# A gather for four heads of 32 tokens, folded by TensorE into 32 output partitions

## The chip, the cores and the metric

One Trainium2 chip, one of its cores, one launch of one program. The time is the device time of that core in microseconds (us). The engines are PE (TensorE, with its weight loads shown apart as PEld), DVE (VectorE), ACT (ScalarE), POOL (GpSimd, which here issues the gathers) and SP (SyncE, which here streams weights and stores results). All of them share 16 DMA engines.

## The reference, cut to what matters

Two transformer blocks run on 512 tokens of width 1024, in float32. The change lies in the end of the second block, a layer of single-neuron experts:

```python
def peer(h, w_query, sub_keys, u_tab, v_tab):        # h [512, 1024], tables [16384, 1024]
    q = (xb @ w_query).reshape(TOKEN_BLOCK, P_HEADS, 2, P_HALF)     # 8 heads, 2 halves of 128
    s = einsum('thpk,hpnk->thpn', q, sub_keys)                      # 128 keys for each half
    sv, si = lax.top_k(s, 16)
    cand = sv[:, :, 0, :, None] + sv[:, :, 1, None, :]              # 16 x 16 candidates
    fv, fpos = lax.top_k(cand, 16)                                  # 16 experts for each token and head
    g = softmax(fv)
    act = gelu(einsum('td,thkd->thk', xb, u_tab[eidx]))             # one dot product for each pick
    return einsum('thk,thkd->td', g * act, v_tab[eidx])             # weighted sum of 128 rows for each token
```

Each of the 512 tokens takes 8 heads x 16 picks = 128 experts, and each pick reads one row of `u_tab` and one of `v_tab` (8 KB together, since the two tables lie side by side). That is 65,536 rows or 537 MB, fetched by 512 gathers of 128 rows.

## The kernel before

The first block runs over all 512 tokens. The second block runs in two halves of 256 tokens, a = 0 and a = 1, and each half goes through the same stages: norm (n1), projections (in2a, in2b), two kinds of attention (mls, dif), output projection (out2), norm (n2), query projection with key scores (pq), and parking of x in DRAM.

The picks of half a can only begin when its key scores exist, at the end of its pq stage. So the 256 gathers of the first half are worked off during the stages of the second half. `picks(a, stage, j)` says how many picks each engine is to have passed before step j of a stage; `PER_US` sets the pace, and `LAST_PICK` = 212 is where the count stops. After the last stage the remaining 300 picks run alone. Every engine executes its program in order, so that a pick's instructions stand between fixed instructions of the stages.

One gather (a "pick", n = 0 to 511) works like this before the change. The 128 tokens of one tile (t = n // 128) sit in the 128 partitions, and pick n brings for each token the row of one head and rank:

- POOL issues the indirect DMA into a row buffer (line 1740). There are 4 buffers for the first 16 picks, 6 up to pick 271, then 8. It waits until the previous user of the buffer is done.
- DVE forms the dot products of 1024 columns with the token's activations (`dot`, line 1559).
- ACT applies Gelu (line 1246) and multiplies by the gate (line 1247).
- The value rows are added with that weight. Even picks (and the first 16) are added by DVE (`value`, line 1573, into `acc`). Odd picks go to PE (line 1053), which needs the weight on a diagonal: ACT makes a 128x128 diagonal (line 1253), and PE multiplies it with the rows in two matmuls of 512 columns, accumulating in PSUM banks 6 and 7. DVE follows its dot products by 1, 2 or 3 picks (`lag_of`); in the stages PE follows by 3 (`BEHIND_PE`).
- After each tile DVE adds both sums, the gate of the block and x, normalizes and lets SP store (`last`, lines 1581 to 1596).

The scores come from PE at line 1162, one head at a time as soon as its two query columns exist. The choice of experts is DVE's: `pick_keys` (lines 1506 to 1518), `pick_pairs` (1523 to 1528), `pick_experts` (1534 to 1544), `pick_gates` (1550, 1551). In half a, `pick_keys` for 14 of the 16 pairs of tile and head stands behind the first 14 picks, one each.

Every fp32 matmul of the program shows in the trace as two MATMUL and two LDWEIGHTS records.

Of the kernel before, what the change touches and what calls it, by code (L numbers as in the profile page):

```python
# [31 lines left out]
P = 128  # L32
# [19 lines left out]
NDIAG = 3  # L52
# [12 lines left out]
def lag_of(n):  # L65
    return 1 if n < NARROW else 2 if n < WIDE else 3


def on_pe(n):
    return n >= NARROW and n % 2 == 1  # L70


TURN, PE_BEFORE, DVE_BEFORE = [0] * NPICK, [0] * (NPICK + 1), [0] * (NPICK + 1)
EXP_AT, ROOT_AT, FETCH_AT, LAST_AT = 9, 14, 1, (3, 6, 8, 10, 16)
PREVIOUS, _seen = [None] * NPICK, {}
for _n in range(NPICK):
# [4 lines left out]
    PE_BEFORE[_n + 1] = PE_BEFORE[_n] + on_pe(_n)  # L81
    DVE_BEFORE[_n + 1] = DVE_BEFORE[_n] + (not on_pe(_n))

STAGES2 = [("n1", 1, 10.0), ("in2a", 17, 3.6), ("mls", 18, 2.5), ("in2b", 12, 3.6), ("dif", 26, 2.2), ("out2", 8, 3.6),
           ("n2", 1, 14.0), ("pq", 20, 3.6), ("park", 1, 4.0)]
# [54 lines left out]
CONSTS = [("ident", 128), ("mask", 512), ("rope", 512), ("sel", 512), ("iota", 16)]  # L140
# [14 lines left out]
def build(nc, ap, out):  # L155
    with ExitStack() as ctx:
        park_x = nc.dram_tensor("park_x", (T, P, D), F32, kind="Internal").ap()
        park_kv = nc.dram_tensor("park_kv", (P, 8 * HALF), F32, kind="Internal").ap()
# [8 lines left out]
        ARENA = 50000  # L167
        whole = sb("whole", [P, ARENA])
        ring = [whole[:, i * BLK:(i + 1) * BLK] for i in range(2)]
        xT = whole[:, 2 * BLK:3 * BLK].rearrange("p (k n) -> p k n", k=KD)  # L170
# [79 lines left out]
        wexp = place(58, 2, NSLOT)  # L250
# [3 lines left out]
        diag = place(62.5, NDIAG, P)  # L254
# [8 lines left out]
        h2tok = place(118, 2, D)  # L263
        acc = place(126, 2, D)
# [87 lines left out]

        def block_arrived(pe, n):
# [7 lines left out]
        def norm_act(act, name, src, n, dst=None, shift=None, ready=None):  # L361

            (b, k), (square, root, _) = NORM0[name], norm_tiles(name)
            for c in range(n):
# [4 lines left out]
                act.activation(square[:, c % 2, :], src(c), ACT.Square).then_inc(nrm_sq, 1)  # L369
# [27 lines left out]
        def norm_dve(dve, own, name, src, n, dst, gain):  # L397
# [7 lines left out]
            for c in range(n):  # L405
                dve.scalar_tensor_tensor(out=dst(c), in0=src(c), scalar=gain(c), in1=root,
# [484 lines left out]
        x_pe, x_parked, x_loaded = sem("x_for_parking"), sem("x_parked"), [sem("x_loaded0"), sem("x_loaded1")]  # L891
# [6 lines left out]
        v_dve, v_pe = sem("values_added_dve"), sem("values_added_pe")  # L898
# [31 lines left out]
        def _(sp):  # L930
# [12 lines left out]
            for t in range(T):  # L943
                sp.wait_ge(fin_ok, t + 1)
                sp.dma_start(out[t * P:(t + 1) * P, :], acc[:, t % 2, :]).then_inc(stored, 16)
# [4 lines left out]
        def _(pe):  # L950
# [91 lines left out]
            def value(n):  # L1042
                if not on_pe(n):
                    return
# [814 lines left out]
```

## Time and profile before

| | |
|---|---|
| median of 3 runs | 3017.92 us (3017.64 to 3023.72) |
| the profiled execution | 3018.04 us, its span 3015.9 us |
| PE busy | 2308.3 us (77%) |
| DVE busy | 1719.9 us (57%) |
| ACT busy | 895.3 us (30%) |
| POOL busy | 655.0 us (22%) |
| gathers and the modulation weights, queue q0 | 587.24 MB, 48.8% of the DMA engines' span |

The page's slices show three regions. Up to about 1400 us the first block and the first half of the second keep PE at 9 tenths while DMA is mostly idle. From about 1450 us all engines share the work and DMA stands at 7 to 9 tenths. In the last quarter PE falls to 5 and 6, DVE stands at 8 and DMA at 9 tenths. DMA's busy share counts the mean of 16 engines; PE's clock is the granted share of full speed. "x" in a row is the number of instructions, and what stands in brackets or behind a bar is the idle time of the engine before them with whoever ended it.

### The profile page before, as it was taken

Reading aid. Unit: us, or ns where it says so; the run is one execution under the profiler, and the core shown is the slowest. Engines: PE = TensorE matmul, PEld = TensorE weight load, DVE = VectorE, ACT = ScalarE, POOL = GpSimd, SP = SyncE. Lnnn points to the kernel's source line nnn. Section 1 sums busy time; section 2 is a strip of 40 time slices with the busy share of each in tenths; the row PEclk is TensorE's granted clock in tenths of the full one; section 3 lists DMA queues with packets and bytes.
Section 4 is the critical chain, followed back from the end, with each engine's and each line's share of the span. In section 5 each row is a group of like instructions: output and inputs, shape, how many; then the busy total and the mean of one; then the engine's idle time right before and its main releaser. Section 6 shows DMA issues by size and latency. Waiting matters only on the chain. (4 is left out here: it accounts for less than half of the span.)

```text
span 3015.9 us, 21942 instructions
## 1 busy us (share of the span) xinstructions
PE 2308.3 (77%) x6878; PEld 1251.0 (41%) x6878; DVE 1719.9 (57%) x3546; ACT 895.3 (30%) x2307; POOL 655.0 (22%) x540
## 2 busy tenths in 40 slices
PE   4999999999999999888475787777754356555555
PEld 2475654644444448667343453445411111111111
DVE  5422226312114314224886867778767888898887
ACT  1012322301000002222256528533322233333332
POOL 0000000000000000000132333333343255545553
PEclk8989989999999998979687797889866677767786
DMA  8520002012117522225598897799998699999998
GB/s 347 205 84 28 29 28 84 29 61 78 70 69 284 189 84 84 94 88 195 196 358 332 325 409 304 311 361 367 379 377 322 237 422 420 413 407 420 411 420 335
DMA packets 93376, 728.23 MB, mean 241 GB/s; under 512 B 10320, under 2 KB 10832, under 8 KB 13264
## 3 DMA queue, kind: packets, MB, share of 16 engines
q0 software_dynamic: 77184, 587.24, 48.8%
q1 hardware_dynamic: 12960, 124.79, 11.1%
q10 hardware_dynamic: 3120, 14.86, 1.3%
q8 instruction: 52, 0.85, 0.1%
q14 instruction: 60, 0.49, 0.0%
HBM read 721.60 MB, written 5.24 MB: 241 GB/s over the span
## 5 line engine op out<-in xcount | busy, mean ns | idle before, releaser
L1053 PE MATMUL PS<-whole 128*128 128x512 f32 x992 | 680.5, 827 | 490.1 <-ACT whole L1253 456.6
L1740 POOL DMA_INDIRECT whole<-in_peer_uv,whole x512 | 641.9, 1254 | 1293.6 <-DVE whole L1573 695.2
L1559 DVE CUSTOM_DVE_ANT_0 whole<-whole 128x1024 f32<-128x1024 f32 x512 | 622.1, 1222 | 252.8 <-DMA whole<-in_peer_uv,whole 246.6
L1053 PEld LDWEIGHTS PS<-whole 128*128 128x128 f32 x992 | 227.3, 251 | 884.5 <-ACT whole L1253 672.7
L452 PE MATMUL PS<-whole 128*128 128x512 f32 (+1 forms) x1072 | 459.1, 587 | 14.8 <-ACT whole L375 6.9
L1083 PE MATMUL PS<-whole 128*128 128x256 f32 x1440 | 341.1, 395 | 33.6 <-ACT whole L1284 24.8
L1246 ACT ACTIVATE whole<-whole 128x1 f32<-128x1 f32 x512 | 103.3, 202 | 821.9 <-DVE whole L1559 815.0
L1573 DVE SCALAR_TENSOR_TENSOR whole<-whole 128x1024 f32<-128x1024 f32 x260 | 333.3, 1282 | 20.0 <-ACT whole L1247 19.9
L1083 PEld LDWEIGHTS PS<-whole 128*128 128x128 f32 x1440 | 287.7, 201 | 100.7 <-issue 50.1
L452 PEld LDWEIGHTS PS<-whole 128*128 128x128 f32 x1072 | 204.3, 192 | 260.2 <-issue 239.8
L1726 POOL DMA_DIRECT2D whole<-in_ada x24 | 12.9, 537 | 1042.7 <-ACTq L343 772.4
L482 PE MATMUL PS<-whole 128*128 128x512 f32 x512 | 222.1, 597 | 6.5 <-ACT whole L375 6.5
L1247 ACT ACTIVATE whole<-whole 128x1 f32<-128x1 f32 x512 | 150.8, 294 | 16.6
L482 PEld LDWEIGHTS PS<-whole 128*128 128x128 f32 x512 | 98.0, 192 | 130.7 <-issue 129.1
L369 ACT ACTIVATE whole<-whole 128x256 f32<-128x256 f32 (+1 forms) x61 | 31.1, 516 | 385.9 <-PE PS L382 226.6
L519 PE MATMUL PS<-whole 64*128 64x128 f32 (+11 forms) x288 | 125.2, 519 | 25.0 <-DVE smalls L726 11.8
L541 PEld LDWEIGHTS PS<-whole 128*128 128x128 f32 x720 | 107.4, 207 | 64.1 <-issue 61.8
L1476 DVE TENSOR_SCALAR whole<-PS 128x512 f32<-128x512 f32 x32 | 22.1, 691 | 196.0 <-PE PS L482 196.0
L840 PE MATMUL PS<-whole 128*128 128x512 f32 x256 | 126.4, 619 | 0.0
L1462 DVE SCALAR_TENSOR_TENSOR whole<-PS,modc,whole 128x512 f32<-128x512 f32 x16 | 12.0, 750 | 189.3 <-PE PS L452 189.3
L541 PE MATMUL PS<-whole 128*128 128x64 f32 (+1 forms) x720 | 106.4, 284 | 13.1 <-DVE whole L781 6.9
L623 DVE CUSTOM_DVE_ANT_0 whole<-PS,whole 128x128 f32<-128x128 f32 (+3 forms) x64 | 31.4, 490 | 130.2 <-PE PS L519 111.9
(249 smaller groups left out, 2162.7 us busy)
## 6 DMA issues: line engine op xcount, KB each, us to landing
whole<-in_wstream SPq DMA_DIRECT2D x32, 2048.0 KB, 7.9
whole<-in_wsecond SPq DMA_DIRECT2D x52, 1024.0 KB, 7.1
whole<-in_ada POOLq DMA_DIRECT2D x24, 2048.0 KB, 8.1
whole<-in_peer_uv,whole POOLq DMA_INDIRECT x512, 9.9
whole<-in_xT ACTq DMA_DIRECT2D x1, 2048.0 KB, 11.0
whole<-in_alibi ACTq DMA_DIRECT2D x1, 2048.0 KB, 8.7
whole<-in_subkeys ACTq DMA_DIRECT2D x2, 1024.0 KB, 7.2
park_x<-whole ACTq DMA_DIRECT2D x4, 512.0 KB
```

The costliest lines, as they stand in the source:

```text
L452: ins = pe.matmul(o, l, r, start=(a == 0), stop=(a == len(lhs) - 1))
L482: ins = pe.matmul(bank(j % 2, n), w[:, k, m * P:(m + 1) * P], act_in(k), start=(k == 0), stop=(k == kc - 1))
L519: ins = pe.matmul(o, l, r, start=True, stop=True)
L541: ins = pe.matmul(o, l, r, start=(a == 0), stop=(a == len(pairs) - 1))
L840: ins = pe.matmul(bank(7), w[:, k, tile(j % 4)], hT[:, k, :], start=(k == 0), stop=(k == KD - 1))
L1053: ins = pe.matmul(bank(6 + b), diag[:, k % NDIAG, :], rows[slot_of(n)][:, D + b * 512:D + (b + 1) * 512], start=opens, stop=closes)
L1083: ins = pe.matmul(bank(q % 2, HALF), w[:, k, tile(c)], src[:, k, :], start=(k == 0), stop=(k == KD - 1))
L1246: own(act.activation(d, d, ACT.Gelu))
L1247: act.activation(w, d, ACT.Copy, scale=gate[:, t % 2, e:e + 1]).then_inc(wexp_ok, 1)
L1559: dve.tensor_tensor_reduce(u, u, h2tok[:, t % 2, :], 1.0, 0.0, ALU.mult, ALU.add, dots[:, e:e + 1]).then_inc(dot_ok, 1)
L1573: dve.scalar_tensor_tensor(out=total, in0=v, scalar=w, in1=total, op0=ALU.mult, op1=ALU.add).then_inc(v_dve, 1)
L1740: pool.indirect_dma_start(rows[j], None, ap["peer_uv"], bass.IndirectOffsetOnAxis(ap=eidx[:, t % 2, e:e + 1], axis=0)).then_inc(landed[j], 16)
```

## The change

A gather now serves four heads of 32 tokens instead of one head of 128 tokens. Partition 32q + i holds token i of the group for head q of a set of four heads. For a tile of 128 tokens there are 8 sets: four token groups times two groups of four heads. Picks n and n+1 (n even) belong to neighbouring sets, that is, to two different token groups.

The weighted sum over picks is then also a sum over the four heads within a gather. ACT builds a 128x32 "fold" matrix for each pick (four 32x32 diagonals under each other, scaled by the weight), and PE multiplies it with the rows into the 32 PSUM partitions of that token group. All picks take this way, and DVE adds no values. The matmuls of picks n and n+1 are issued as a pair, in alternation.

What goes with it:

- `sub_scores` writes the scores in the new layout, with 16 matmuls of 32 output partitions for each set, and a set needs the query columns of four heads. `SCORE_AT` puts these after steps 9 to 12 and 17 to 20 of pq, which has 24 steps instead of 20.
- The dot products need each token's activations in four copies. They are written to DRAM (`park_h`) and read back in pieces of two groups (`load_h`, 8 DMAs of 32 rows on ACT's queue, 1 MB together).
- In the second half `pick_keys` stands once in 16 picks (`KEYS_AT`) instead of behind each of the first 14.
- `VBANK` puts the third tile's sum into banks 4 and 5; the first step of `last` comes at pick 5 of the next tile instead of 3, and `last` has one step less.
- POOL waits for PE alone before it reuses a buffer; a pair of picks is released together.
- x lies as `x4`, half by half.

The core of the diff (what else changes follows from it):

```diff
-NDIAG = 3
+NDIAG = 8
-def on_pe(n):
-    return n >= NARROW and n % 2 == 1
+def set_of(e):
+    return 2 * (e // 32) + e % 2
+def rank_of(e):
+    return e % 32 // 2
+def group_of(v):
+    return 2 * (v // 4) + v % 2
+SCORE_AT = [9, 10, 11, 12, 17, 18, 19, 20]
+VBANK = [6, 6, 4, 6]
+for _v in range(3, 2 * PH):
+    _b = PK * (_v - 2) - 8
+    KEYS_AT[_b], PAIRS_AT[_b + 4], EXPERTS_AT[_b + 8], EXPS_AT[_b + 11], GATES_AT[_b + 14] = _v, _v, _v, _v, _v
...
         def picks(a, stage, j, behind=0):
-        return max(0, min(j - 9, (j - 5) // 2, EARLY_PICKS)) if stage == "pq" else 0
+        return max(0, min(j - 15, EARLY_PICKS)) if stage == "pq" else 0
...
             def value(n):                                   # on PE
-                if not on_pe(n):
+                if n % 2 == 0:
                     return
-                pe.wait_ge(diag_ok, k + 1)
+                pe.wait_ge(diag_ok, n + 1)
...
                 for b in range(2):
-                    ins = pe.matmul(bank(6 + b), diag[:, k % NDIAG, :], rows[slot_of(n)][:, D + b * 512:D + (b + 1) * 512],
-                                    start=opens, stop=closes)
+                    for m in (n - 1, n):
+                        j = 32 * group_of(set_of(m % NSLOT))
+                        ins = pe.matmul(PS[j:j + 32, VBANK[t] + b, :], diag[:, m % NDIAG, :],
+                                        rows[slot_of(m)][:, D + b * 512:D + (b + 1) * 512],
+                                        start=m % NSLOT % 64 < 2, stop=m % NSLOT % 64 > 61)
                 ins.then_inc(v_pe, 1)
...
+            def sub_scores(a, i):
+                v = SCORED[i]
+                j, g = group_of(v), v % 4 // 2
+                for c in range(4):
+                    tl, p = c // 2, c % 2
+                    tokens = slice(P * tl + 32 * j, P * tl + 32 * j + 32)
+                    for q in range(4):
+                        k = 2 * (4 * g + q) + p
+                        ins = pe.matmul(PS[32 * q:32 * q + 32, 2 + i % 4, tile(c)], pqt[a][:, k, tokens], skw[:, k, :],
+                                        start=True, stop=True)
+                return ins
...
             def weight(n):                                  # on ACT
-                if on_pe(n):
...
-                    act.activation(diag[:, k % NDIAG, :], ident, ACT.Copy, scale=w).then_inc(diag_ok, 1)
+                act.activation(diag[:, n % NDIAG, :], const("fold"), ACT.Copy, scale=w).then_inc(diag_ok, 1)
...
+                if n % 64 == 2 and n // 64 + 1 in (2, 3, 5, 6, 7):
+                    load_h(n // 64 + 1)
...
-            def value(n):                                   # on DVE, taken out
-                    dve.scalar_tensor_tensor(out=total, in0=v, scalar=w, in1=total, op0=ALU.mult, op1=ALU.add).then_inc(v_dve, 1)
...
                 m = PREVIOUS[n]                             # on POOL
-                if m is not None and on_pe(m):
-                    pool.wait_ge(v_pe, PE_BEFORE[m] + 1)
-                elif m is not None:
-                    pool.wait_ge(v_dve, DVE_BEFORE[m] + 1)
+                if m is not None:
+                    pool.wait_ge(v_pe, m // 2 + 1)
```

The instructions move as follows. First PE in the pq stage of the first half, before the change: L1083 is the query projection (8 matmuls for each step), L1162 the scores of a head, L1061 the turning of x.

```order
L1083 MATMUL PS<-whole 128x256 x32
L1162 MATMUL PS<-whole 128x128 x4
L1083 MATMUL PS<-whole 128x256 x16
L1162 MATMUL PS<-whole 128x128 x4
L1083 MATMUL PS<-whole 128x256 x16
```

The same place after the change, where L1119 is the projection, L1096 the scores of a set and L1075 a pair of picks:

```order
L1119 MATMUL PS<-whole 128x256 x80
L1096 MATMUL PS<-whole 32x128 x16
L1119 MATMUL PS<-whole 128x256 x8
L1096 MATMUL PS<-whole 32x128 x16
L1119 MATMUL PS<-whole 128x256 x8
L1096 MATMUL PS<-whole 32x128 x16
L1119 MATMUL PS<-whole 128x256 x8
L1096 MATMUL PS<-whole 32x128 x16
L1119 MATMUL PS<-whole 128x256 x24
L1075 MATMUL PS<-whole 32x512 x4
L1096 MATMUL PS<-whole 32x128 x32
```

The first scores stand behind ten steps of the projection instead of four, and each set has 16 matmuls where a head had 4.

Second, DVE at the end of the program, before the change: L1559 is the dot product (two rows each, the second reads its sum), L1573 the adding of values, L1581 to L1596 the closing of the tile.

```order
L1559 ISA whole<-whole 128x1024
L1559 ISA whole 128x1
L1559 ISA whole<-whole 128x1024
L1559 ISA whole 128x1
L1573 SCALAR_TENSOR_TENSOR whole<-whole 128x1024 x2
L1581 TENSOR_TENSOR whole<-whole,PS 128x1024
L1584 TENSOR_TENSOR whole<-whole 128x1024
L1587 TENSOR_TENSOR whole<-whole 128x1024
L1589 ISA whole,smalls<-whole 128x1024
```

And after it, where L1603 is the dot product and L1611 to L1617 the first steps of the closing:

```order
L1603 ISA whole<-whole 128x1024
L1603 ISA whole 128x1
L1603 ISA whole<-whole 128x1024
L1603 ISA whole 128x1
L1611 TENSOR_TENSOR whole<-PS,whole 128x1024
L1615 TENSOR_TENSOR whole<-whole 128x1024
L1617 ISA whole,smalls<-whole 128x1024
```

DVE has only dot products left for a pick, and one full-width instruction less in the closing.

## Rows read from the trace of the kernel before

**Rows 1.** Stretches: busy us (instructions) of each engine, PE clock, DMA share, GB/s.
```profile
core 0: us, PE busy (x) PEld busy (x) DVE busy (x) ACT busy (x) POOL busy (x), PEclk, DMA share, GB/s
1500.00:2200.00 700.00, 502.51 (x1648) 311.61 (x1648) 541.00 (x1076) 347.71 (x813) 240.35 (x206) 0.84 0.88 350
2300.00:2400.00 100.00, 37.00 (x44) 12.15 (x44) 82.95 (x308) 20.56 (x61) 24.27 (x24) 0.64 0.61 230
2440.00:3016.00 576.00, 323.85 (x448) 104.88 (x446) 485.35 (x824) 194.55 (x609) 295.65 (x218) 0.75 0.98 405
1826.00:1942.00 116.00, 77.45 (x259) 43.34 (x259) 87.53 (x169) 81.40 (x161) 34.60 (x31) 0.78 0.72 277
```
**Rows 2.** Stretches, dot products alone (line 1559), two records for each.
```profile
1480.00:2280.00 800.00, 291.20 (x477) 0.81 0.89 350
2280.00:2440.00 160.00, 53.59 (x89) 0.68 0.76 293
2440.00:3016.00 576.00, 271.07 (x444) 0.75 0.98 405
```
**Rows 3.** Waits from 1500 to 2200 us: total us, times, longest.
```profile
POOL whole L1740 <- DVE whole L1573: 297.5, 86, 11.6
POOL whole L1740 <- PE PS L1053: 134.1, 45, 11.2
PE PS L1053 <- ACT whole L1253: 119.5, 37, 16.2
```
**Rows 4.** Groups from 1500 to 2200 us: busy us, mean ns, idle before.
```profile
L1053 PE MATMUL PS<-whole 128*128 128x512 f32 x400 | 240.2, 733 | 126.3 <-ACT whole L1253 119.5 <-DVE whole L1581 5.1 <-issue 1.6
L1573 DVE SCALAR_TENSOR_TENSOR whole<-whole 128x1024 f32<-128x1024 f32 x104 | 133.2, 1281 | 19.9 <-ACT whole L1247 19.9
L1253 ACT ACTIVATE whole<-cst,whole 128x128 f32<-128x128 f32 x100 | 40.2, 402 | 3.3
L1247 ACT ACTIVATE whole<-whole 128x1 f32<-128x1 f32 x206 | 60.7, 294 | 6.7
```
**Rows 5.** Instructions in order of time: start us, us, instruction, count, idle before.
```profile
2504.80 1.98 PE L1053 MATMUL PS<-whole 128*128 128x512 f32 x4 [1.70 <-ACT whole L1253]
...
2505.34 0.19 PEld L1053 LDWEIGHTS PS<-whole 128*128 128x128 f32 x1 [0.24 <-issue]
...
2505.77 0.19 PEld L1053 LDWEIGHTS PS<-whole 128*128 128x128 f32 x1 [0.24 <-issue]
```
**Rows 6.** PE in order of time, picks alone, 2509 to 2519 us.
```profile
2509.76 3.78 PE L1053 MATMUL PS<-whole 128*128 128x512 f32 x4 [2.97 <-ACT whole L1253]
2514.73 3.78 PE L1053 MATMUL PS<-whole 128*128 128x512 f32 x4 [1.20 <-ACT whole L1253]
```
**Rows 7.** PE in order of time, mls stage, all 128 rows.
```profile
1667.10 0.83 PE L541 MATMUL PS<-whole 128*128 128x128 f32 x6
1667.77 1.02 PE L519 MATMUL PS<-whole 128*128 128x512 f32 x2
1668.63 0.60 PE L529 MATMUL PS<-cst,whole 128*128 128x128 f32 x4
```
**Rows 8.** PE in order of time, dif stage, L519 on 64 of the rows.
```profile
1857.57 0.83 PE L541 MATMUL PS<-whole 128*128 128x128 f32 x6
1858.33 1.12 PE L519 MATMUL PS<-whole 64*128 64x512 f32 x2
1859.38 0.55 PE L529 MATMUL PS<-cst,whole 128*128 128x128 f32 x3
```
**Rows 9.** PE and POOL in order of time, pq stage of the first half.
```profile
1376.97 15.10 PE L1083 MATMUL PS<-whole 128*128 128x256 f32 x64
1391.91 1.05 PE L1162 MATMUL PS<-whole 128*128 128x128 f32 x8
1392.80 7.07 PE L1083 MATMUL PS<-whole 128*128 128x256 f32 x32
...
1406.31 0.99 POOL L1740 DMA_INDIRECT whole<-in_peer_uv,whole  x1 [350.26 <-DVE whole L1544]
```
**Rows 10.** DVE, PE and ACT's queue in order of time, end of the program.
```profile
3000.71 1.23 DVE L1559 CUSTOM_DVE_ANT_0 whole<-whole 128x1024 f32<-128x1024 f32 x1 [1.22 <-DMA whole<-in_peer_uv,whole]
...
3002.60 0.33 ACTq L1238 DMA_DIRECT2D whole<-park_x  x1
...
3007.19 1.23 DVE L1584 TENSOR_TENSOR whole<-whole 128x1024 f32<-128x1024 f32 x1
```

More of the change, by code:

```diff
@@ L249, in build @@
         gate = place(57, 2, NSLOT)
-        wexp = place(58, 2, NSLOT)
+        wexp = place(58, NSLOT)
         cand = place(59, PK * PK)
@@ L350, in bank, with two @@
             return PS[rows, b, 0:n]
+        def two(a):
+            return a.rearrange("p (a n) -> p a n", a=2)
         def block_arrived(pe, n):
@@ L1152, in _ @@
                         features(PQ + j, h2T)
-                    if 3 <= j < 19 and j % 2 == 1:
-                        h = (j - 3) // 2
-                        pe.wait_ge(ev2, first + PQ + 2 * h + 2)
-                        if h == 0:
-                            pe.wait_ge(tt_ev, 2 + a)
-                        if h >= 4:
-                            pe.wait_ge(pk_ev, PH * a + h - 3)
-                        for c in range(4):
-                            tl, p = c // 2, c % 2
-                            ins = pe.matmul(PS[:, 2 + h % 4, tile(c)], pqt[a][:, 2 * h + p, tile(tl)], skw[:, 2 * h + p, :],
-                                            start=True, stop=True)
-                        ins.then_inc(sk_done, 1)
+                    if j in SCORE_AT:
+                        i = SCORE_AT.index(j)
+                        pe.wait_ge(ev2, first + PQ + (8 if i < 4 else 16))
+                        if i == 0:
+                            pe.wait_ge(tt_ev, 2 * a + 2)
+                        if i >= 4:
+                            pe.wait_ge(pk_ev, PH * a + i - 3)
+                        sub_scores(a, i).then_inc(sk_done, 1)
                 pe.wait_ge(pk_ev, PH * (a + 1))
                 for tl in range(2):
-                    turn(xT, tile(2 * a + tl), 2 + 2 * tl).then_inc(x_pe, 1)
-            values.to(NPICK // 2 + 32)
-            turn(h2T, tile(1), 0).then_inc(tt_pe, 1)
+                    turn(x4[:, a], tile(tl), 2 + 2 * tl).then_inc(x_pe, 1)
             values.to(NPICK)
@@ L1235, in fetch_x, with load_h @@
             def fetch_x(t):
                 act.wait_ge(x_parked, 16 * (t + 1))
-                act.wait_ge(dot_ok, NSLOT * (t + 1))
-                act.dma_start(h2tok[:, t % 2, :], park_x[t]).then_inc(x_loaded[t % 2], 16)
+                if t > 0:
+                    act.wait_ge(fin_ms, t)
+                act.dma_start(xrow, park_x[t]).then_inc(x_loaded, 16)
+            def load_h(f):
+                t = f // 2
+                act.wait_ge(h_parked[t % 2], 16 * (t // 2 + 1))
+                if f >= 2:
+                    act.wait_ge(dot_ok, 64 * (f - 1))
+                for i in range(2):
+                    g = 32 * (2 * (f % 2) + i)
+                    for q in range(4):
+                        act.dma_start(h2rep[32 * q:32 * q + 32, 2 * (f % 2) + i, :], park_h[t, g:g + 32, :]).then_inc(h_loaded[f % 2], 16)
@@ L1588, in last @@
+                    dve.tensor_scalar(ssf[:, 0:1], ssf[:, 1:2], 1.0 / D, EPS, ALU.mult, ALU.add).then_inc(fin_ms, 1)
                 if step == 3:
[L1589 to L1591 removed]
                     dve.wait_ge(fin_rt, t + 1)
```

244 lines of the change are left out of this document (118 added, 126 removed).

## The prediction

> **What bounds the kernel now.** I read the page's slices first, then a table of stretches, then the waits. The reader is to see two regimes in which picks are worked off.
>
> In the last one, from 2440 us on, the DMA engines are 0.98 busy at 405 GB/s, while DVE has 485 of 576 us and PE 324 [rows 1]. 444 records are 222 dot products [rows 2], so a pick takes 576 / 222 = 2.59 us with the closing of the program in it. At the 420 GB/s that the page's slices reach, one gather of 1.05 MB takes 2.5 us. Here DMA is the bound, and work taken off DVE buys nothing.
>
> From 1500 to 2200 us the picks share the engines with the stages of the second half. DMA is 0.88 busy, DVE 541 of 700 us, PE 503, ACT 348 [rows 1]. The 477 records from 1480 to 2280 us are about 239 dot products, 3.35 us each [rows 2]. No engine is full; the waits show a ring: POOL waits 297.5 us for DVE's adding of values and 134.1 us for PE's before it may reuse one of six buffers, and PE waits 119.5 us for the diagonal of a pick [rows 3]. In between lies a stretch of its own: from 2300 to 2400 us DMA is 0.61 busy while DVE is 0.83 busy with 308 short instructions [rows 1], the 14 key searches in a row.
>
> So at most three things can be won: the idle DMA time of the shared regime, 0.12 x 700 = 84 us; that of the key stretch; and the closing.
>
> **The change part by part**, against the profiled execution's 3018.04 us (span 3015.9 us; the runs' median is 3017.92 us, the same for this purpose).
>
> 1. *Later first gather.* Before, PE has done four projection steps when it scores head 0, and 64 records take 1391.91 - 1376.97 = 14.9 us [rows 9]. Now ten steps come first: 6 x 3.73 = 22 us later. The DVE chain from scores to experts and the gathers behind it stay as long. The 8 early picks stand after steps 16 to 23 instead of 10 to 19, with four buffers, and the second half can start only behind them. During this time DMA is mostly idle and nothing hides the delay. I take +22 us; +5 if the early picks catch up, +45 if the scores below cost their worst.
>
> 2. *Scores.* A head's 8 records take 1392.80 - 1391.91 = 0.89 us [rows 9], 0.11 us each. A set has 32 records. If the four neighbouring matmuls (four output groups) run at once, a set takes about 0.9 us and 8 sets cost what 8 heads did; one after another it is 3.6 us, 8 x 2.7 = 21 us more in each half. I take +4 for the first half; in the second the picks lie beside it.
>
> 3. *DVE loses the values.* 104 instructions of 1.28 us, 133 us of the shared regime [rows 4]; DVE falls from 541 to about 408 us of 700. This shortens the ring for even picks. Odd ones, which went by PE already, held the ring as well [rows 3], and now every buffer goes that way, with the even one waiting for its partner.
>
> 4. *PE takes all values.* 400 records, 100 picks, were busy 240 us [rows 4]. A pair of picks had 4 records and now has 8. With the clock at full speed 4 records take 1.98 us [rows 5], at the half-speed level 3.78 us [rows 6]. No column tile of this width runs beside another anywhere in this trace, so the cost is bounded: side by side, 8 records take the time of 4 to 5 (the pair's two records are in order, so the first and the last have no partner), 240 to 270 us in all; one after another, twice, 480 us, or 390 if the clock stays at full speed (100 times two blocks of 1.98 us). I take side by side, 4.5 slots: +30 us of PE, since the two go to different 32-column groups of the array.
> TensorE: Matmul & The Clock Gate in the Trainium skill ("Measured speedup vs the span model") gives 2.38x for three column tiles of 512 columns, which would speak for this; no run here shows it yet.
> Changing the array's shape costs something, too. A full-height block of six records and one of two take 0.67 and 0.86 us from start to start [rows 7]; with the second on 64 rows they take 0.76 and 1.05 us [rows 8], 0.28 us for going there and back. At some 100 pairs that is 28 us of PE. PE comes to 503 + 58 = 561 of 700 us and keeps its slack.
> By TensorE: Matmul & The Clock Gate in the Trainium skill (Part 3, "What overlaps and what doesn't") a weight load overlaps a running matmul only when the row groups differ. Here all use all rows; yet the loads of 2505.34 and 2505.77 us lie inside a matmul block of 1.98 us [rows 5], so for full-height weights the trace disagrees. By the rule, eight loads of 0.19 us each would add 1.5 us to a pair, some 150 us of PE; it is part of the slower rival.
>
> 5. *ACT.* 100 diagonals of 0.402 us become 206 of 128x32. The nearest rows are 0.294 us for one column and 0.402 for 128 [rows 4]; at 0.32 that is 66 us instead of 40, +26 us. Between 1826 and 1942 us ACT has 81 of 116 us [rows 1], DMA only 0.72, so what DVE gains is partly not usable there. Five of eight `load_h` fall behind picks, 8 issues of 0.33 us each [rows 10], 2.6 us a time; four of them 64 picks apart, covered by the buffers.
>
> 6. *The shared regime together.* Of 84 us idle DMA I let half come back, 42 us, since PE and ACT remain in the ring. Against it stand some 4 MB more (h parked and reloaded) at 420 GB/s, 10 us. At picks 128 to 133 PE waits for the closing of tile 0, which DVE reaches after dot product 133, the last that six buffers allow, so DMA drains once: 4 us. Net -28 us. Bounds: -74 us (all but the extra bytes), +95 us (serial columns, below).
>
> 7. *Keys spread.* From 2280 to 2440 us 89 records are about 45 dot products [rows 2]; at 2.5 us they would take 112, so 48 us are lost. One key search in 16 picks leaves DVE below 2.5 us a pick. I take -43; bounds -48 and 0.
>
> 8. *The DMA-bound end.* Three `load_h` more, 1 MB each: +7 us. The last closing loses one instruction of 1.23 us [rows 10], and the last pair may take PE a little longer: 0, bounds -1 and +4.
>
> Sum: +22 + 4 - 28 - 43 + 7 = -38 us, 2980 us. The halving in part 6 is the softest number; DVE gets a quarter of its time back, and a ring of six buffers gets less jitter than the average shows, so I put 10 us more there: 2970 us.
>
> **The rivals.**
> *The columns don't run side by side* (slower). Place: every pair on PE in the shared regime. PE then has 503 + 150 to 240 + 28 = 681 to 771 us of work, beside the 78 us that it idles for other reasons than picks (700 - 503 - 119 [rows 1, 3]). A PE so busy should keep its clock high: the other 263 us at full instead of 0.84 speed are 42 less. The stage then takes 681 - 42 + 78 = 717 us at the least, and near 795 in the middle of both ends without that help: +17 to +95, and I take +50. With +22, +15 for scores, -43 and +7 this is 3069 us. It decides from about 6 record times per pair upwards. For it: nothing in the trace shows two matmuls side by side. Against it: PE's slack of 200 us, and in the end regime 7.6 us a pair at half speed [rows 6] would turn into 4.0 [rows 5] once PE is busy throughout, under the 5.0 us that DMA needs.
> *The shared regime is bound by its chains* (scores, weighing, exponent, turning) and not by DVE's load. Speaking for it: the 1826 stretch. Then part 6 gives +4 and the total is 3018 + 22 + 4 + 4 - 43 + 7 = 3012 us, no change by measure.
> *DMA fills up fully.* Part 6 at -74, part 1 at +5 with the early picks hidden: 3018 + 5 + 4 - 74 - 48 + 7 = 2912 us. For it: 0.98 in the end regime with the same gathers.
>
> **How the numbers follow.** Forecast family (2940 to 2995 us) 0.48, around 2912 us 0.14, chains 0.14, serial columns 0.24. A measurement of this kernel can tell about 0.2% (6 us) from no change. Faster: 0.48 + 0.14 + half of chains 0.07 = 0.69; same: 0.06; slower: 0.25. The range: the low end 2900 us takes in the full-DMA case; the high end 3065 us takes in half of the serial case, leaving some 0.12 above and 0.05 below. The likeliest case's own range is 2940 to 2995 us.
>
> **What would show it.** First gather at about 1428 us instead of 1406. In PE's order of time a block of 8 records of the pairs taking about 2.2 us at full clock (right) or 3.6 (serial). Stage of the second half ending near 2170 us instead of about 2185 in spite of the later start. DMA share above 0.92 there. No stretch under 0.9 between 2280 and 2440 us. A rate of 2.5 us a pick from there on, unchanged. The prediction is wrong if the pair's block takes 6 or more record times, or if DMA's share in the shared regime stays at 0.88.

## The result and the profile after

The changed kernel takes 3053.47 us (median of 4 runs, 3046.25 to 3057.28) against 3020.21 us of the kernel before in the same sessions (3017.64 to 3023.72): a ratio of 1.0107, 95% interval 1.0082 to 1.0131. It is 1.1% slower. Faster by 38 to 48 us was forecast. Its profiled execution has a span of 3044.2 us, 28.3 us more than before.

One thing has to be known before single traces are compared. The query projection of the first half stands before every changed pick. In the five traces of the old code and its variants it begins between 1370.3 and 1379.2 us, in the twelve of the new code between 1368.2 and 1379.5 us. So a trace can be 10 us early or late before the change does anything. Of the two compared here, the one after is 8.8 us early (1368.18 us against 1376.97 us [rows 9]).

The two executions are best compared by when DVE begins the same dot product; this table is read from DVE's rows in order of time (lines 1559 and 1603).

| dot product | before, us | after, us | after minus before |
|---|---|---|---|
| 0 | 1415.1 | 1432.4 | +17.3 |
| 16 | 1517.9 | 1530.2 | +12.3 |
| 64 | 1686.3 | 1709.7 | +23.4 |
| 128 | 1905.2 | 1928.7 | +23.5 |
| 224 | 2216.8 | 2269.3 | +52.6 |
| 256 | 2307.8 | 2357.6 | +49.8 |
| 272 | 2386.8 | 2410.1 | +23.3 |
| 511 | 3000.7 | 3031.3 | +30.6 |

So the start cost 12 us in this table, and 21 us counted from the start of the query projection. The shared regime lost 40 us more (picks 16 to 224), where a gain of 28 us was forecast. The stretch of the key searches (256 to 272) won 26.5 us; the DMA-bound end lost 7.3 us; and the closing won some 2 us. The 40 us is at the upper end: the old code's picks 16 to 224 took 699 us here, but 708 and 707 us in the traces of two variants that change nothing before pick 220, and the new code's 739 to 742 us in four with pairs. The loss is 31 to 43 us.

The same stretches as in [rows 1], of the changed kernel:

```profile
1500.00:2200.00 700.00, 515.23 (x2198) 263.00 (x2202) 404.15 (x958) 365.38 (x883) 209.16 (x194) 0.84 0.85 334
2300.00:2400.00 100.00, 50.73 (x136) 8.33 (x136) 52.32 (x108) 32.51 (x109) 37.84 (x34) 0.71 0.97 365
```

DVE fell from 541 to 404 us, just as its lost instructions say, and PE rose by only 13 us. Yet DMA moved 334 instead of 350 GB/s, and POOL issued 194 gathers instead of 206. Every engine has time to spare and the picks are slower. The dot products alone, answering to [rows 2]:

```profile
1480.00:2280.00 800.00, 269.90 (x440) 0.83 0.84 331
2280.00:2440.00 160.00, 65.34 (x107) 0.73 0.96 367
2440.00:3016.00 576.00, 274.00 (x448) 0.75 1.01 413
```

That is 220 instead of 239 dot products in the first stretch and about 54 instead of 45 in the second. The waits from 1500 to 2200 us say who is short of what, against [rows 3]:

```profile
POOL whole L1766 <- PE PS L1075: 479.3, 89, 29.8
DVE whole L1603 <- DMA whole<-in_peer_uv,whole: 269.1, 137, 8.9
PE PS L1075 <- ACT whole L1292: 107.2, 37, 13.8
```

Before, POOL's 432 us of waiting were split between DVE (297.5) and PE (134.1). Now all 479 us are waits for PE, and DVE waits 269 us for rows to land. In the same stretch before, DVE waited 114.5 us for them:

```profile
DVE whole L1559 <- DMA whole<-in_peer_uv,whole: 114.5, 75, 4.5
```

DVE is early and has nothing to do, because the buffers are not free.

The amount of PE's work is not the trouble. Groups of the same stretch, against [rows 4], and two blocks in order of time, a pair of picks (L1075) and the scores of a set (L1096):

```profile
L1075 PE MATMUL PS<-whole 128*32 128x512 f32 x776 | 231.2, 727 | 122.9 <-ACT whole L1292 107.2 <-DVE whole L1611 15.4
L1292 ACT ACTIVATE whole<-cst,whole 128x32 f32<-128x32 f32 x194 | 62.4, 321 | 6.4
```
```profile
1866.39 1.91 PE L1075 MATMUL PS<-whole 128*32 128x512 f32 x8
1868.23 0.94 PE L561 MATMUL PS<-whole 128*128 128x128 f32 x6
```
```profile
1403.68 1.08 PE L1096 MATMUL PS<-whole 128*32 128x128 f32 x32
```

Eight records of a pair take 1.91 us where four took 1.98 [rows 5], and 32 score records of four column groups take 1.08 us where 8 took 1.05 [rows 9]. The 776 records of twice as many matmuls are busy 231 us, less than the 400 before (240 us).

One place costs more than the average shows. When the first tile ends, the second tile's sum uses the same PSUM banks as the first's, so PE may not open it before DVE has taken the first one. That step now stands behind pick 5 of the next tile instead of pick 3:

```profile
1953.24 7.20 PE L1075 MATMUL PS<-whole 128*32 128x512 f32 x24 [15.43 <-DVE whole L1611]
```

PE idled 5.1 us there before [rows 4, for L1581]. Dot products 128 to 136 take 40.1 us instead of 30.5 us; in the traces of all twelve versions of the new kernel they take 35 to 42 us, in those of the old one without pairs 29 to 31 us. So some 5 to 12 us of the shared regime's loss lie here. No run moves this step, so its share of the whole time is not shown.

The first ten steps of the projection, then the first gather, POOL in order of time:

```profile
1368.18 35.57 PE L1119 MATMUL PS<-whole 128*128 128x256 f32 x160
1418.30 0.99 POOL L1766 DMA_INDIRECT whole<-in_peer_uv,whole  x1 [372.02 <-DVE whole L1588]
```

The first gather comes 12 us later than in [rows 9], but 50.1 us after the projection's start instead of 29.3 us. That is 21 us more. From the projection's start to the first gather the twelve traces of the new code have 49.5 to 50.2 us and the five of the old one 28.5 to 29.3 us.

### The profile page after: what moved, and what is told of

Its sections match the earlier page's. It is cut to its first block, busy times and chain, and to the rows that moved or that the text cites. A ratio compares the mean times of both kernels' runs of the same rounds, so it can differ in the third digit from the quotient of the medians.

```text
span 3044.2 us, 24894 instructions
## 1 busy us (share of the span) xinstructions
PE 2322.1 (76%) x8318; PEld 1128.1 (37%) x8318; DVE 1412.8 (46%) x3278; ACT 959.5 (32%) x2570; POOL 573.6 (19%) x540
## 4 chain that ended last, share of the span: by engine, by line
PE 53%; DMA 24%; DVE 13%; ACT 5%; issue 3%; POOL 2%; ACTq 0%; POOLq 0%; DVEq 0%
DMA whole<-in_peer_uv,whole 23%; PE PS L472 14%; PE PS L1075 9%; PE PS L502 7%; PE PS L1119 7%; DVE whole L1603 4%; PE PS L860 4%; PE PS L539 3%; PE PS L561 2%; PE PS L549 2%; POOL whole L1766 2%; PE PS L401 1%; PE PS L882 1%; PE PS L1126 1%; PE PS L1013 1%
## 5 line engine op out<-in xcount | busy, mean ns | idle before, releaser
L1075 PE MATMUL PS<-whole 128*32 128x512 f32 x2048 | 688.2, 813 | 536.5 <-ACT whole L1292 507.2
L1603 DVE CUSTOM_DVE_ANT_0 whole<-whole 128x1024 f32<-128x1024 f32 x512 | 623.9, 1225 | 584.7 <-DMA whole<-in_peer_uv,whole 582.1
L1766 POOL DMA_INDIRECT whole<-in_peer_uv,whole x512 | 560.5, 1095 | 1411.7 <-PE PS L1075 940.3
L1075 PEld LDWEIGHTS PS<-whole 128*32 128x32 f32 x2048 | 121.9, 133 | 1028.4 <-ACT whole L1292 742.5
L1119 PE MATMUL PS<-whole 128*128 128x256 f32 x1440 | 340.6, 395 | 2.9 <-ACT whole L1328 1.6
L1119 PEld LDWEIGHTS PS<-whole 128*128 128x128 f32 x1440 | 279.9, 198 | 90.6 <-issue 50.3
L472 PEld LDWEIGHTS PS<-whole 128*128 128x128 f32 x1072 | 204.0, 192 | 261.3 <-issue 241.9
L502 PE MATMUL PS<-whole 128*128 128x512 f32 x512 | 222.6, 598 | 6.5 <-ACT whole L394 6.5
L1292 ACT ACTIVATE whole<-cst,whole 128x32 f32<-128x32 f32 x512 | 164.5, 321 | 16.8
L502 PEld LDWEIGHTS PS<-whole 128*128 128x128 f32 x512 | 98.2, 192 | 131.0 <-issue 129.4
L561 PEld LDWEIGHTS PS<-whole 128*128 128x128 f32 x720 | 104.6, 204 | 64.5 <-issue 59.7
L860 PE MATMUL PS<-whole 128*128 128x512 f32 x256 | 122.2, 602 | 0.0
L645 ACT ACTIVATE whole<-whole,smalls 128x128 f32<-128x128 f32 (+3 forms) x96 | 53.9, 561 | 163.9 <-DVE smalls L643 163.8
```

The lines of the kernel that those rows point to most:

```text
L472: ins = pe.matmul(o, l, r, start=(a == 0), stop=(a == len(lhs) - 1))
L502: ins = pe.matmul(bank(j % 2, n), w[:, k, m * P:(m + 1) * P], act_in(k), start=(k == 0), stop=(k == kc - 1))
L561: ins = pe.matmul(o, l, r, start=(a == 0), stop=(a == len(pairs) - 1))
L860: ins = pe.matmul(bank(7), w[:, k, tile(j % 4)], hT[:, k, :], start=(k == 0), stop=(k == KD - 1))
L1075: ins = pe.matmul(PS[j:j + 32, VBANK[t] + b, :], diag[:, m % NDIAG, :], rows[slot_of(m)][:, D + b * 512:D + (b + 1) * 512], start=m % NSLO ...
L1119: ins = pe.matmul(bank(q % 2, HALF), w[:, k, tile(c)], src[:, k, :], start=(k == 0), stop=(k == KD - 1))
```

## The experiments

The theory: in the shared regime the bound is the ring of six row buffers. POOL issues gathers in order and waits for each buffer. Before, an even pick's buffer came free as soon as DVE had added it, 2 picks behind; now it comes free only with its odd partner and only by PE, which stands between stage work. The rivals: the column groups don't run side by side, the extra DMA traffic (h written and read back), DVE's load, PE's lag. Where a trace is compared below, its own early or late start is taken out by counting from dot product 16. Each run was timed against the kernel before on the same chip; ratios are to that.

### The release in pairs, alone, in the kernel before

```diff
                 elif m is not None:
                     pool.wait_ge(v_dve, DVE_BEFORE[m] + 1)
+                    if on_pe(m + 1):
+                        pool.wait_ge(v_pe, PE_BEFORE[m + 1] + 1)
```

> The kernel before, with one thing of the change alone: POOL may reuse the buffer of an even pick only when PE has also done its odd partner (DVE adds even values as ever). If the shared regime is held by the ring of six buffers and the release in pairs is what made it slower, dot product 224 comes 25 to 50 us later than in the kernel before (2217 us) and the whole takes 3040 to 3065 us. If the release is harmless and the loss lies in the extra DMA traffic, in ACT's or in PE's added work, the time stays within 6 us of 3020.

Measured: 3074.52 us, ratio 1.0167 (1.0109 to 1.0225), 55 us slower and beyond the 3040 to 3065 us named. In its trace dot product 16 comes 7 us earlier than before, which is that trace's early start; 224 comes 54 us later, and from 272 on the distance stays at 58 to 60 us. From dot product 16 to 224 it takes 760 us, against 699 to 708 us in three traces without the added wait: 52 to 61 us more. The waits from 1500 to 2200 us:

```profile
POOL whole L1742 <- PE PS L1053: 334.5, 58, 18.0
DVE whole L1559 <- DMA whole<-in_peer_uv,whole: 181.3, 82, 7.1
POOL whole L1742 <- DVE whole L1573: 119.2, 31, 8.9
```

One added wait moves POOL's waiting from DVE to PE and starves DVE's dot products, the picture of the changed kernel. The loss ends where eight buffers and no stage work follow. In the kernel before, the release alone costs more than the changed kernel lost.

### PE closer to the picks

```diff
-BEHIND_ACT, BEHIND_PE = 1, 3
+BEHIND_ACT, BEHIND_PE = 1, 1
```

> The changed kernel with PE following the picks by 1 instead of 3 in the stages. If the ring is the bound, buffers come free about two picks earlier, DMA's share in the shared regime rises above 0.85 and dot product 224 comes 20 to 50 us earlier than 2269 us: 3000 to 3030 us. If PE's own stage work is the bound, PE now waits more for diagonals inside the stages and the time is the same or up to 30 us longer.

Measured: 3130.60 us, ratio 1.0358 (1.0305 to 1.0411), 77 us slower than the changed kernel. The expectation of the ring theory failed: dot product 224 comes 79 us later, not 20 to 50 us earlier. That of PE's waiting held, though the loss is more than twice the 30 us named. PE's wait from 1500 to 2200 us:

```profile
PE PS L1075 <- ACT whole L1292: 200.7, 72, 10.3
```

PE waits 201 instead of 107 us for diagonals, and stage work stands behind these waits in its program: from 1500 to 2200 us ACT waits 153 us for PE's projections (L1119), where it waited 24 us in the changed kernel. POOL still waits 507 us for PE. So asking PE for a buffer earlier in its program didn't free it earlier here.

### The extra loads cut to 32 KB

```diff
     ...
-    act.dma_start(h2rep[32 * q:32 * q + 32, ...], park_h[t, g:g + 32, :])
+    m = 32 if f < 2 else 1
+    act.dma_start(h2rep[32 * q:32 * q + m, ...], park_h[t, g:g + m, :])
```

> The changed kernel with the six later loads of the activations cut from 1 MB to 32 KB each (one row of 32; the dot products then use partly stale activations). If the extra traffic costs what its bytes cost, the DMA-bound end gains 7 us (three loads) and the shared regime 5 to 8 us: 3038 to 3045 us. If the loads stall the ring by more than their bytes, dot product 224 comes 20 us or more earlier and the whole is below 3030 us.

The dot products that then use stale activations take as long as before, and so this run shows the time of the traffic alone.

Measured: 3029.86 us, ratio 1.0018 (0.9994 to 1.0041), 24 us less than the changed kernel. That is more than the 12 to 15 us of the bytes and on the border of the second answer, but dot product 224 doesn't come 20 us earlier: in this trace, which starts 9.8 us later, it is 2.4 us ahead. Counted from dot product 16 it is 13 us ahead at 224 and 27 us at the end, of which 10 us come after dot product 272. The traffic costs 24 to 27 us in all. Both parts cost more than their bytes: 13 instead of 5 to 8 us in the shared regime, 10 instead of 7 us in the end.

### The key searches spread, alone, in the kernel before

```diff
-                if i < 2 * PH - 2:
+                head = base + 2 + i // PK
+                if base == 0 and i < 2 * PH - 2:
                     pick_keys((base + 2 + i) // PH, (base + 2 + i) % PH)
+                if base > 0 and i % PK == 0 and i // PK + 2 < 2 * PH:
+                    pick_keys(head // PH, head % PH)
```

> The kernel before with the key searches of the second half spread, one in 16 picks, nothing else. If these searches alone starve DMA from 2300 to 2400 us, the kernel gains 25 to 45 us: 2975 to 2995 us. If the stretch is slow for another reason (the change of the buffers' order at pick 272, the closing of tile 1), it gains less than 10 us.

Measured: 3004.07 us, ratio 0.9945 (0.9922 to 0.9968), 16 us faster: between the two answers. From dot product 224 to 272 it takes 141 us instead of 170 us, the same 141 us as the changed kernel. From 272 to 511 it gives 10 us back. A likely reason, not tested here: DVE, which still adds values, now searches keys while DMA is the bound (DVE had 485 of 576 us there already [rows 1]).

### Part of DVE's load put back

```diff
+                if n % 2 == 0 and n % 64 != 0:
+                    hr = h2rep[:, 2 * (f % 2) + n % 2, :]
+                    own(dve.tensor_scalar(hr, hr, 1.0, None, ALU.mult))
                 dve.wait_ge(landed[slot_of(n)], 16 * (TURN[n] + 1))
```

> The changed kernel with a full-width DVE instruction of about the length of an added value (the activations times 1.0, in place) before the dot product of each even pick but the first of each 64, so that DVE carries the load that the change took off it. If DVE's load was never what held the shared regime, dot product 224 stays within 15 us of the changed kernel's 2269 us and the whole within 15 us of 3053. If the relief of DVE did win something that the pair release hid, the whole is 30 to 60 us longer.

Measured: 3063.22 us, ratio 1.0146 (1.0117 to 1.0175), 10 us more than the changed kernel, with intervals that overlap a little. In its trace dot product 224 is 11 us later, 5 us counted from dot product 16. But the added instruction is not of the length of an added value. From 1500 to 2200 us:

```profile
L1602 DVE TENSOR_SCALAR whole<-whole 128x1024 f32<-128x1024 f32 x93 | 64.6, 694 | 0.1
```

It takes 0.69 us where the adding took 1.28 us [rows 4], and DVE is busy 461 us in this stretch: 57 of the 137 us that the change took off are back, under half. So this run says that 57 us of DVE work cost about 10 us. If the cost grows evenly with the work, the whole relief is worth some 25 us; that is an estimate from this one point, and no run put the full load back.

### Another order of the four matmuls

```diff
-                for b in range(2):
-                    for m in (n - 1, n):
+                for m in (n - 1, n):
+                    for b in range(2):
```

> The changed kernel with the four matmuls of a pair in another order: both halves of the even pick, then both of the odd one, so that neighbours mostly lie in the same array columns. If running side by side depends on alternating column groups, a pair's block takes 3.0 to 3.6 us at full clock instead of 1.91 us, PE gets 100 us and more of work in the shared regime and the whole takes 3080 to 3150 us. If the order doesn't matter, nothing moves by more than 6 us.

Measured: 3053.89 us, ratio 1.0110 (1.0077 to 1.0143): nothing moves. A block at full clock (granted share 1.00):

```profile
2518.38 1.92 PE L1075 MATMUL PS<-whole 128*32 128x512 f32 x8 [1.72 <-ACT whole L1292]
```

The alternation buys nothing; 8 records still take 1.92 us. This alone left open whether there is any running side by side, or whether a narrow matmul is just faster.

### Both picks in the same columns

```diff
-                        j = 32 * group_of(set_of(m % NSLOT))
+                        j = 32 * (group_of(set_of(m % NSLOT)) // 2 * 2)
```

with the accumulation opened and closed by one of the pair.

> The changed kernel with both picks of a pair in the same 32 array columns (their token groups are then added together and the other columns' results are missing). If neighbouring column groups run side by side, this takes that away: a pair's block takes 3.4 to 3.7 us at full clock instead of 1.91 us, and the whole 3090 to 3170 us. If a matmul with 32 stationary columns is simply twice as fast as one with 128, the block stays at 1.9 us and the time at 3053 us.

Measured: 3121.00 us, ratio 1.0344 (1.0322 to 1.0367), 67 us more than the changed kernel. A block of a pair at full clock (granted share 1.00 from 2501 to 2505 us):

```profile
2501.33 3.62 PE L1075 MATMUL PS<-whole 128*32 128x512 f32 x8 [1.21 <-ACT whole L1292]
```

3.62 against 1.91 us: the gain comes from the two column groups, in either order of issue. The clock must be looked at in such a comparison, since at a granted clock of 0.50 a pair side by side takes 3.62 us as well (the changed kernel at 1860.09 us). The rival of the serial columns is false for the changed kernel. Its price can be checked here: the prediction put the shared regime 78 us apart between serial (+50) and side by side (-28), and dot products 16 to 224 take 51 us longer in this run, the whole 67 us.

### The two extra buffers earlier

```diff
-NARROW, WIDE = 16, NPICK // 2 + 16
+NARROW, WIDE = 16, 220
```

in the changed kernel, and in the kernel before with spread keys.

> The changed kernel with the two extra row buffers in use from pick 226 on instead of 278, and the order of the buffers kept even where the count changes (at pick 220). If buffers are what keeps DMA under its best rate between 2200 and 2440 us, dot product 288 comes 10 to 20 us earlier: about 3038 us. If not, no change.

> The kernel before with spread key searches (3004 us in its own run) and in addition the two extra row buffers from pick 226 on. The same reasoning: 8 to 20 us less than with spread keys alone, 2984 to 2996 us, if the ring holds DMA there; 3000 to 3007 us if it doesn't.

Measured: 3029.80 us (1.0038, 1.0022 to 1.0054), 24 us less than the changed kernel; and 2984.55 us (0.9876, 0.9852 to 0.9899), 20 us less than spread keys alone. In the changed kernel's version nothing moves up to dot product 224; at 288 it is 17 us ahead and stays so. With every engine's work the same, just the stretch with the new buffers gets faster: the ring again.

This edit does two more things. With the switch at pick 272, gather 272 needs the buffer of pick 268, only four picks before it, and POOL waits 16.9 us there in the kernel before (5.3 us in the changed one); with the switch at 220 no gather from there on needs a buffer used fewer than six picks before. And in the kernel before `lag_of` takes the same limit, so that DVE adds values 3 instead of 2 picks behind from pick 220 on. In the changed kernel 8 of the 17 us are there at dot product 256, before the old switch, and these belong to the buffers; the other 8 us can be either. In the kernel before the parts are not separated.

### Each pick released by itself

PE takes one pick at a time and POOL waits for that pick; ACT's and DVE's counts follow.

```diff
-                if n % 2 == 0:
-                    return
...
-                    for m in (n - 1, n):
+                    for m in (n,):
...
-                    pool.wait_ge(v_pe, m // 2 + 1)
+                    pool.wait_ge(v_pe, m + 1)
```

> The changed kernel, but PE takes each pick by itself and POOL reuses a buffer as soon as its own pick is added; nothing else of the change is undone. If the release in pairs is what the shared regime lost (61 us when it alone was put into the kernel before), dot product 224 comes 30 to 50 us earlier than 2269 us and the whole takes 3005 to 3025 us. If the picks can't run side by side any more when they are handed over one by one, PE is busier and the gain is below 15 us.

Measured: 3006.69 us, ratio 0.9957 (0.9939 to 0.9975), 47 us less than the changed kernel and 0.4% faster than the kernel before. The stretch from 1500 to 2200 us:

```profile
1500.00:2200.00 700.00, 570.48 (x2240) 275.41 (x2239) 422.36 (x1013) 376.07 (x907) 218.26 (x198) 0.93 0.87 343
```

In its trace dot product 224 comes 15 us earlier than in the changed kernel's, and the last 30 us earlier, though this trace starts 11 us later. Counted from dot product 16 it is 26 us ahead at 224 and 40 us at the end, near the 47 us of the timed runs. It shows one more thing: PE is busy 570 instead of 515 us, and the granted clock is 0.93 instead of 0.84. A single pick mostly runs alone, and its four records take at full clock as long as the eight of a pair:

```profile
2724.05 1.90 PE L1073 MATMUL PS<-whole 128*32 128x512 f32 x4 [0.58 <-ACT whole L1290]
```

The gain could thus have come from PE. The next run took the release back and kept the rest.

```diff
-                    pool.wait_ge(v_pe, m + 1)
+                    pool.wait_ge(v_pe, m // 2 * 2 + 2)
```

> PE takes each pick by itself, as in the single-release kernel (3007 us), but POOL reuses a buffer only when the pair is done, as in the changed kernel (3053 us). If the release is the cause, the time goes back to 3040 us or more although PE works as in the single-release kernel. If the gain of single release came from PE (it starts the even pick earlier, and its granted clock was 0.93 instead of 0.84 in the shared regime), the time stays at 3005 to 3020 us.

Measured: 3045.87 us, ratio 1.0087 (1.0059 to 1.0115). The stretch:

```profile
1500.00:2200.00 700.00, 567.15 (x2137) 274.23 (x2140) 406.67 (x964) 372.06 (x890) 209.17 (x192) 0.91 0.84 330
```

PE's work and clock stay about as they were, DMA falls back to 330 GB/s, and 39 of the 47 us are lost again. The release is the cause of these 39 us. The other 8 us are not clear of noise (1.0087 against 1.0107, with overlapping intervals).

With the single release the changed kernel takes 3007 us, and the kernel before with nothing but spread key searches takes 3004 us. All else that the change brought makes no gain together.

### Single release with the early buffers, and PE's lag once more

The same with `WIDE = 220`, and that with `BEHIND_PE = 4`.

> Single release and in addition the two extra buffers from pick 226 on, which gave the changed kernel 23 us by itself. If both add up: 2985 to 3000 us, faster than the kernel before (3020 us). If they draw on the same idle DMA time: 3005 us or more.

> The same with PE following the picks by 4 instead of 3 in the stages. With 1 instead of 3 the changed kernel lost 77 us, since PE waited for diagonals inside the stages. If that wait still counts at 3, 4 gains 5 to 20 us more; if the ring of six buffers counts more, 4 loses 10 us or more.

Measured: 3002.30 us (0.9948, 0.9931 to 0.9965) and 3035.71 us (1.0054, 1.0038 to 1.0071). The first lies between its two answers. The early buffers add 4 us, within the noise, not the 24 us that they gave the changed kernel: both draw on the same idle DMA time for the most part. The trace of this execution ends 20 us before the other, but 17 us of that are there at dot product 224, where the two programs are still the same; after it the early buffers win 3 us. A lag of 4 costs 33 us more: with the 77 us for a lag of 1 (in the version with pairs) it brackets 3.

### The keys in the changed kernel, and an earlier release on DVE

```diff
-    KEYS_AT[_b], PAIRS_AT[_b + 4], ... = _v, _v, _v, _v, _v
+    KEYS_AT[_v - 3], PAIRS_AT[_b + 4], ... = _v, _v, _v, _v, _v
```

> The changed kernel with the second half's key searches behind the first 13 picks again, one each; nothing else. In the kernel before, spreading them alone was worth 27 us at pick 272 and 16 us at the end. If the same holds here, the time is 3065 to 3080 us. If the lighter DVE hides the searches by itself, 3053 to 3058 us, and then this part of the change bought nothing.

Measured: 3070.54 us, ratio 1.0159 (1.0135 to 1.0184), 17 us more than the changed kernel. In its trace, which starts 11 us late, dot product 224 is 11 us behind the changed kernel's and 272 is 28 us behind. The lighter DVE doesn't hide 13 searches in a row.

```diff
-    return 1 if n < NARROW else 2 if n < WIDE else 3
+    return 1 if n < WIDE else 3
```

in the kernel before with spread keys and early buffers.

> The kernel before with spread keys and the early extra buffers (2985 us), and DVE adding an even pick's values one pick behind its dot product instead of two while there are six buffers. If an earlier release alone helps the ring, 2970 to 2980 us. If DVE then waits for ACT's weight (some 1.3 us of Gelu and gate, more where ACT loads a table) and its stage work comes later, 2990 us or more.

Measured: 2981.61 us, ratio 0.9868 (0.9848 to 0.9889), against 0.9876 without it. It lies between the two answers and the intervals overlap: no gain is shown. A possible reason, not tested: PE's odd picks hold the ring at a lag of 3, so that the even ones can't free it further.

The fastest versions are thus the kernel before with spread keys and early buffers: 1.2 to 1.3% faster than the kernel before, 2.3 to 2.4% faster than the changed one, without any of the new layout.

## Why the prediction was wrong

The step that failed is in part 3: that an even pick has to wait for its odd partner, and that every buffer now comes free by PE, was named and priced at nothing. The runs put 39 to 55 us on it, and that turned the sign.

- *Parts 1 and 2, later start:* +22 and +4 us forecast. From the projection's start the first gather came 21 us later and dot product 16 came 21 us later. Right, and only the early start of this one trace makes it look like 12 us. The second half's first norm came 24 us later in the table's sense and 33 us counted from the projection. A set of scores takes 1.01 us from start to start against 0.89 us for a head, almost nothing, as taken.
- *Part 3, DVE loses the values:* the load fell as worked out (404 us against 408). What failed is the clause "Odd ones, which went by PE already, held the ring as well [rows 3], and now every buffer goes that way, with the even one waiting for its partner". It named the mechanism and priced it at nothing. Alone it costs 55 us (b_pair), and taking it out of the changed kernel gives 47 us, 39 of them by the release alone (a_single, a_latefree). This is the step that turned the sign.
- *Part 4, PE takes all values:* 8 records in the time of 4.5 were forecast; it was 4 (1.91 us). PE came to 515 us, not 561. The price of changing the array's shape, 28 us, is in these 561; no run separates it. By TensorE: Matmul & The Clock Gate in the Trainium skill (Part 3, "What overlaps and what doesn't"), which the prediction cites, a weight load overlaps a running matmul only when the row groups differ. The trace after disagrees as the one before did: 8 loads lie in the 1.91 us, all on the same rows.
- *Part 5, ACT:* 0.321 us for a 128x32 diagonal, 0.32 taken. Right.
- *Part 6, the shared regime:* -28 us forecast, +31 to +43 measured. The halving of the idle DMA share was a number without a mechanism, and the share did not rise at all: it fell from 0.88 to 0.85, which is one of the prediction's own signs of being wrong. Against the forecast stand the release (39 to 55 us), the traffic in this stretch (13 us, 10 taken) and the closing of tile 0 (PE idle for 15.4 us, 4 taken). DVE's relief gave 10 us for under half of it, where 42 us were taken for the whole. The 10 us that were put on top for "less jitter" had nothing under them.
- *Part 7, keys:* -43 us forecast, -26.5 in the trace, -17 by its own experiment. All of the stretch's loss was put down to the searches. But the changed kernel, with no searches in a row, still made only 54 dot products in 160 us, not 64. The switch of the buffers at pick 220 instead of 272 wins 17 us more there (a_wide), so buffers held it too.
- *Part 8, the DMA-bound end:* +7 forecast, +7.3 measured, and partly luck. The three loads cost 10 us there (a_noh) and the spread searches 5 us (from dot product 272 on, a_keysbunch takes 617 us and the changed kernel 621 us); some 7 us came back from something that no run isolates. The closing: -2.
- *The rivals:* 3053 us lies inside the stated range of 2900 to 3065 us, but that is luck. The high end was there for half of the serial case, and the columns do run side by side. Its sum has a slip as well: without the clock's help the middle of its two ends is 804 us, not 795. "The shared regime is bound by its chains" was nearest, and it was allowed no loss.

Not settled: the parts don't add up. Start 21, release 39 to 55, traffic 24 to 27, DVE's relief -10 to -25 and keys -16 to -17 give 42 to 77 us for the measured 33, so they overlap; and the b_pair figure holds in a kernel where DVE still adds values.

## What to carry to other kernels

When several engines share a ring of buffers, ask of a change first what it does to the moment at which each buffer comes free, and only then what it takes off an engine; where transfers are issued in order, the buffer that comes free last holds up the ones behind it. A wait that stands in the middle of an engine's program is not moved up for free: placed earlier here, it stalled the stage work behind it and cost 77 us. An idle share of a resource is no gain until a mechanism says who will use it; test that by one added wait or by added buffers in the old kernel. Here the added wait took two lines and gave the sign and a size of 55 us. When load is put back as a test, measure the instruction that puts it back: here it took 0.69 us where 1.28 us was meant. And before two traces are compared, find a point ahead of the change and see how far apart they are already.

## What the runs showed of the hardware

- Two fp32 matmuls with 128 rows and 32 columns each run side by side in two column groups: 8 records of 512 columns in 1.91 us, against 3.62 us in the same columns, both at a granted clock of 1.00. The 4 records of one pick alone take 1.90 us, so 32 columns are not faster than the 128 of [rows 5] (4 records in 1.98 us). With four groups, 32 records of 128 columns take 1.08 us, where 8 records of full width take 1.05 us [rows 9]. The order in which they are issued made no difference (1.91 and 1.92 us).
- PE's granted clock from 1500 to 2200 us was 0.84 with pairs (515 us busy) and 0.93 with the same matmuls one pick at a time (570 us busy). It bought nothing clear of noise here: with the late release the time was 3046 us at 0.91, against 3053 us.
- A high busy share of the DMA engines isn't full rate. From 2300 to 2400 us they were busy 0.97 at 365 GB/s with six buffers in the changed kernel, and 1.01 at 405 GB/s with eight (a_wide).
- The length of a full-width fp32 instruction on DVE depends on its kind: the scaling of 128x1024 in place took 0.69 us, the adding with a weight 1.28 us [rows 4], the dot product 1.22 us.
